# Router, slot table and first weight units reordered in a one-core retention, latent-attention and expert trunk

## The reference, cut to what matters

```python
# h_res: 16 meta tokens + 256 frames, D_MODEL 1024, two layers, float32
for layer in range(2):
    hn = rms_norm(h_res, attn_norm[layer])
    r_q, r_k, r_v, r_g, c_q, c_kv, k_rope = split(hn @ w_in[layer])
    y_ret = head_rms(retention(rope(r_q) * 128**-0.5, rope(r_k), r_v)) * ret_out_gain[layer] * silu(r_g)
    y_mla = head_rms(latent_attention(c_q, c_kv, k_rope, ...)) * mla_out_gain[layer]
    h_res = h_res + concat([y_ret, y_mla]) @ w_out[layer]
    hn = rms_norm(h_res, ffn_norm[layer])
    if layer == 0:
        h_res = h_res + (silu(hn @ w_gate) * (hn @ w_up)) @ w_down          # D_FF 3584
    else:
        top_val, top_idx = top_k(hn @ router_w, 2)                          # 8 experts
        gates = softmax(top_val)
        for e in range(8):
            h_res = h_res + gate_dense[:, e] * (silu(hn @ w_gate[e]) * (hn @ w_up[e])) @ w_down[e]
out = rms_norm(h_res, final_norm)[:, 16:]
```

## Time and profile before

| | us |
|---|---|
| median of 3 runs | 1513.21 (1512.12 to 1514.98) |
| profiled execution, its own time | 1514.2 |
| its span, first to last instruction | 1512.4 |
| PE busy | 1486.0 (98%) |
| DVE / ACT / POOL busy | 1229.4 / 1007.2 / 44.3 |
| 16 transfer engines moving | 445.89 MB, mean 295 GB/s |
| chain that ended last | PE 92%, DVE 4%, ACT 2%, DMA 1%, issue 1% |

### The profile page before, as it was taken

The page is one execution under the profiler, slowest core; times in us unless marked ns, Lnnn a source line. Parts: engine busy times, 40 slices in busy tenths (PEclk is TensorE's granted clock), DMA queues, the critical chain, the costliest instruction groups (busy, mean ns, idle before and its releaser), DMA issues.

```text
span 1512.4 us, 21641 instructions
## 1 busy us (share of the span) xinstructions
PE 1486.0 (98%) x8278; PEld 1289.0 (85%) x8278; DVE 1229.4 (81%) x1055; ACT 1007.2 (67%) x939; POOL 44.3 (3%) x44
## 2 busy tenths in 40 slices
PE   9999999999999999999999999999999999999997
PEld 8779999999988888888888888888888888888885
DVE  6746776777784678888898898888889888888887
ACT  7656433333575567777777777777777777777775
POOL 0000000000000031000000000000000000000000
PEclk9999999999999999999999999999999999999999
DMA  9305544444323469999999999999999999999992
GB/s 356 123 36 223 194 168 172 185 174 167 124 106 141 168 228 391 383 369 402 380 350 403 379 348 403 391 345 393 398 349 383 400 377 353 408 373 345 421 383 101
DMA packets 64857, 445.89 MB, mean 295 GB/s; under 512 B 8137, under 2 KB 8169, under 8 KB 12832
## 3 DMA queue, kind: packets, MB, share of 16 engines
q1 hardware_dynamic: 61344, 435.39, 73.4%
q0 software_dynamic: 3456, 9.71, 2.3%
HBM read 440.10 MB, written 7.36 MB: 296 GB/s over the span
## 4 chain that ended last, share of the span: by engine, by line
PE 92%; DVE 4%; ACT 2%; DMA 1%; issue 1%; SPq 0%; DVEq 0%; ACTq 0%
PE bank L524 89%; PE bank L528 3%; DVE w_lo L1320 1%; DMA ring<-stream 1%; ACT w_hi L998 0%; DVE scratch L1382 0%; ACT scratch L1076 0%; DVE scratch L1378 0%; DVE scratch L1367 0%; DVE scratch L1371 0%; ACT scratch L1075 0%; DVE scratch L1384 0%; DVE scratch L1527 0%; DVE scratch L1647 0%; DVE w_lo L1655 0%
## 5 line engine op out<-in xcount | busy, mean ns | idle before, releaser
L524 PE MATMUL bank<-w_hi,parts 128*128 128x512 f32 x2688 | 833.7, 391 | 1.5 <-issue 0.8
L1655 DVE TENSOR_TENSOR w_lo<-ring,w_hi 128x2048 fp32r<-128x2048 f32 x285 | 653.3, 2292 | 87.6 <-ACT w_hi L1220 84.2
L1220 ACT ACTIVATE w_hi<-ring 128x2048 fp32r<-128x2048 f32 x285 | 546.9, 1919 | 173.7 <-PE bank L524 146.4
L524 PEld LDWEIGHTS bank<-w_hi,parts 128*128 128x128 f32 x2688 | 500.3, 188 | 103.5 <-DVE w_lo L1655 1.1
L524 PE MATMUL bank<-w_lo,parts 128*128 128x512 f32 x1344 | 523.7, 390 | 0.0
L524 PE MATMUL bank<-parts,w_hi 128*128 128x272 f32 (+1 forms) x2240 | 427.3, 289 | 2.0 <-DVE w_lo L1320 1.9
L524 PEld LDWEIGHTS bank<-parts,w_hi 128*128 128x128 f32 x2240 | 351.6, 188 | 4.3 <-DVE w_lo L1320 2.5
L524 PE MATMUL bank<-parts,w_lo 128*128 128x272 f32 (+1 forms) x1120 | 321.3, 287 | 0.0
L524 PEld LDWEIGHTS bank<-w_lo,parts 128*128 128x128 f32 x1344 | 252.3, 188 | 53.1
L524 PEld LDWEIGHTS bank<-parts,w_lo 128*128 128x128 f32 x1120 | 211.0, 188 | 0.3
L1320 DVE TENSOR_TENSOR w_lo<-ring,w_hi 128x2048 fp32r<-128x2048 f32 x72 | 163.5, 2288 | 49.4 <-ACT w_hi L998 49.3
(11 more groups left out here) (187 smaller groups left out, 626.6 us busy)
## 6 DMA issues: line engine op xcount, KB each, us to landing
ring<-stream SPq DMA_DIRECT2D x357, 1024.0 KB, 6.1
hT<-stream SPq DMA_DIRECT2D x48, 1024.0 KB, 6.5
ring<-stream SPq DMA_DIRECT2D x4, 512.0 KB, 5.6
ring<-stream SPq DMA_DIRECT2D x2, 976.0 KB, 4.6
ring<-stream SPq DMA_DIRECT2D x2, 768.0 KB, 11.6
c_sb<-consts SPq DMA_DIRECT2D x1, 1136.0 KB, 11.1
hT<-h SPq DMA_DIRECT2D x4, 272.0 KB, 6.2
ring<-stream SPq DMA_DIRECT2D x2, 544.0 KB, 6.1
```

The lines of the kernel that those rows point to most:

```text
L524: return release(nc.tensor.matmul(dst, lhsT, rhs, start=start, stop=stop), inc)
L1220: A(w_hi[:, n % HSLOTS, :], moe_slot(m), ACT.Copy).then_inc(split_hi, 1)
L1655: V.tensor_tensor(w_lo[:, n % HSLOTS, :], moe_slot(m), w_hi[:, n % HSLOTS, :].bitcast(F32), ALU.subtract).then_inc(split_lo, 1)
```

## The change

It has four parts.

1. **Start.** Unit 1 is loaded, rounded and subtracted in two halves, as unit 0 was (`load_half(u, j)`, `high_half`, `low_half`), and PE's `cq0` begins on the first half. Unit 2 is loaded ahead of the constants. `keep_clock` is 21 instead of 24.
2. **Both attentions.** `square_sum` follows `cq1` instead of `cq0`, ACT evicts `cq0` and `cq1` before `row_root`. `low(b+6)` and `low(b+7)` leave the run of ropes: one goes behind `rope(10)`, one between the first two `mask_max`. `high(b+7)` goes behind `v2`. The fold of the eight squares is made in another order (`half_squares` first).
3. **Router.** The slot table has a third word, the token's 1/rms; `hn_rows` holds `res` without it, POOL's two multiplications and `hn_tok` are gone, and in passes 1 to 7 the scale enters in `Silu(scale=norm_now)` and in DVE's product (`scalar_tensor_tensor` with `slot_norm`); for pass 0 it is 1, since `G` holds 1/rms. ACT copies the scale of a pass to `norm_now` and waits for that. ACT squares the last two token blocks straight from PSUM before it copies them. DVE makes `G` and `G_last` before `gained(1)`, and takes the first rows (`take(0)`) ahead of the gate arithmetic. The counts of all experts go to bank 3 with a semaphore of their own (`total_done`). `keep_clock(5, 3)` stands before the counting and `keep_clock(2, 6)` behind it. POOL clears `x_rows` after two copies instead of four. `wo(7)` is parted in two with `logits(6, 7)` between. `scatter_copy` moves from the head of a pass to the end of the pass before, and falls away for pass 0.
4. **End.** The last two down units are used one by one, both halves of columns for each. The two last additions go before `fin_eps`; the last store is issued by ACT.

```diff
@@ SP, start @@
-            load_half(0)
+            load_half(0, 0)
             load_rows(0)
             load_rows(1)
-            load_half(1)
+            load_half(0, 1)
             load_rows(2)
             load_rows(3)
-            load(1)
+            load_half(1, 0)
+            load_half(1, 1)
+            load(2)
             sp.dma_start(c_sb[:, :], consts).then_inc(const_in, 16)
-            load(2)
...
@@ POOL, router @@
-            pool.wait_ge(tok_free, 4)
+            pool.wait_ge(tok_free, 2)
             nc.gpsimd.memset(x_rows, 0.0).then_inc(rows_set, 1)
             pool.dma_start(fn_sb, fnorm[:, 0, :]).then_inc(fn_in, 16)
             pool.wait_ge(gained_ready, 4)
-            pool.wait_ge(r_ready, 1)
-            for t in range(2):
-                nc.gpsimd.tensor_tensor(hn_tok[:, t, :], res[:, t, :], dev_tok[:, t, 3:4].to_broadcast([P, D]),
-                                        ALU.mult).then_inc(tokhn_ready, 1)
...
@@ PE, end of layer 1's attention @@
-                    wo(7, [*latent, *retained], True)
-                    logits(6, 8)
+                    wo(7, latent, False)
+                    logits(6, 7)
+                    wo(7, retained, True)
+                    logits(7, 8)
                     turn_tokens(1)
...
@@ ACT, turn_copies @@
+                copy(0)
+                copy(1)
+                square(0)
+                square(1)
+                A(warm[:, :], eps_sb[:, :], ACT.Sqrt)
+                square(2)
+                square(3)
+                copy(2)
                 act.wait_ge(tok_sum, 1)
                 A(dev_tok[:, :, 2:3], dev_tok[:, :, 2:3], ACT.Sqrt, bias=eps_sb[:, 0:1], scale=1.0 / D).then_inc(tok_std, 1)
+                copy(3)
...
@@ ACT, expert @@
-                scatter_copy(it)
+                A(norm_now[:, 0:1], slot_norm[:, it, :], ACT.Copy).then_inc(norm_set, 1)
+                act.wait_ge(norm_set, it + 1)
...
-                        A(sil_moe, bank[c % 2][:, :], ACT.Silu).then_inc(e_silu, 1)
+                        A(sil_moe, bank[c % 2][:, :], ACT.Silu, scale=norm_now[:, 0:1]).then_inc(e_silu, 1)
...
+                if not final:
+                    scatter_copy(it + 1)
...
@@ DVE, expert @@
-                        V.tensor_tensor(a_moe, bank[2 + c % 2][:, :], sil_moe, ALU.mult).then_inc(e_af, 1)
+                        V.scalar_tensor_tensor(out=a_moe, in0=bank[2 + c % 2][:, :], scalar=slot_norm[:, it, :], in1=sil_moe,
+                                               op0=ALU.mult, op1=ALU.mult).then_inc(e_af, 1)
...
@@ PE, last pass @@
                 def down_by_halves():
-                    for half in range(2):
-                        for f in range(4):
-                            i = f // 2
...
+                    for i in range(2):
+                        w = [x.rearrange("p (f n) -> p f n", f=2) for x in ready(("d", c, i))]
+                        for half in range(2):
+                            for ff in range(2):
```

175 lines of the change are left out of this document (95 added, 80 removed).

## The result

The changed kernel takes 1500.65 us (median of 4 runs, 1500.11 to 1501.44), the kernel before, run beside it, 1512.66 (1511.83 to 1514.98). The ratio is 0.9919, 95% interval 0.9901 to 0.9936: 0.8% faster. The profiled executions have spans of 1498.8 and 1512.4, 13.6 us apart; 1.5 us of that is the profiled execution of before, which took 1514.2 and so lay that far above its median.

What follows compares the result with a forecast made beforehand. PE, busy 1486.0 of 1512.4 us, was taken as the bound, so only its idling and low clock could be won. 5.0 + 0.7 + 1.9 + 1.9 + 2.8 + 0.4 = 12.7 us, from 1513.2 to 1500.5; range 1497.5 to 1505.0.

Steps and rivals of the forecast that it cites:

- Layer 0, start and ropes: Layer 0's attention: 1.3 us from an earlier root, 2.2 and 1.54 from moving two subtractions out of the ropes; 5.0 us.
- a lead for PE only: Layer 0's start: `cq0` starts about 1.9 us earlier, but DVE's unit 3 rest still stands behind `row_scale` and `rope(0)`.
- PE's wait before q2: Layer 0: PE stands still some 1.3 us before q2, costing nothing since the ropes end the stretch.
- Before the dense layer: Sum of squares before the dense layer: ready at 154.05 instead of 154.8; taken as 0.7 us, between 0 and 1.4.
- Layer 1's ropes: Layer 1's attention: 2.2 + 1.57 us from two moved subtractions, less 1.85 for the later root; gain 1.9 us.
- Layer 1's clock: Behind layer 1's ropes: with two of three waits gone PE's clock does not fall; 1.9 us, between 0 and 1.9.
- Router: Routing up to unit 3's rest in the first pass, which ends at 558.3 instead of 561.1; gain 2.8 us, bounds 0.9 to 4.2.
- The memset's term: Router: POOL's memset now runs beside DVE's `gained(0)`; cost taken as 0, at most 0.7 us.
- Passes: Expert passes: DVE's product at 0.74 instead of 0.68 us and ACT's new copy are both hidden; cost 0.
- End: Kernel's end: the 0.7 us wait for the last `w_lo` goes, second rest gains 0.3; taken as 0.4, -0.3 to 0.9.
- low clock stays: Layer 1's ropes and the gather keep the low clock, each costing 1.9 us: gain 8.9, time 1504.3; chance 0.20.
- The rival of the late unit 2: Start: unit 2 still lands at 19.7, root 1.2 us later, not 1.3 earlier: gain 10.2, time 1503.0; chance 0.10.

Runs made afterwards that it cites:

- e1: Changed kernel with both subtractions, `low(b + 6)` and `low(b + 7)`, put back among the ropes of both layers: 1511.03 us, ratio 0.9975 to before.
- e11: Changed kernel with unit 1 loaded, rounded and subtracted as a whole again, unit 2 still ahead of the constants: 1505.39 us, ratio 0.9940 to before.
- e4: Changed kernel with the sum of squares between cq0 and cq1 again and the root ahead of their evictions, both layers: 1498.76 us, ratio 0.9900 to before.
- e2: Changed kernel with only the first subtraction, `low(b + 6)`, put back among the ropes, in both layers: 1505.01 us, ratio 0.9944 to before.
- e10: Changed kernel with the last two down units used by halves of columns again: 1502.61 us, ratio 0.9921 to before.
- e9: Changed kernel with the last two additions of the residual behind `fin_eps` again: 1501.90 us, ratio 0.9918 to before.
- e5: Changed kernel without the seven matmuls of ones in the router: 1502.81 us, ratio 0.9927 to before.
- e3: Changed kernel with the constants loaded ahead of unit 2 again: 1505.11 us, ratio 0.9935 to before.

## Why the prediction was right

It named 1500.5 us and 12.7 us of gain; measured were 1500.65 and, between medians, 12.0, between the profiled spans 13.6. Term by term, against the marks:

- **Layer 0, start and ropes, 5.0.** Measured 5.02. The parts are 1.6 (start, said 1.3) and 3.4 (two subtractions, said 2.2 + 1.54 = 3.74); e1 gives the 3.4 back. Two errors of 0.3 cancel. One sentence of this step was wrong: that unit 1 in halves is a lead for PE only. With the sum behind cq1 the root needs that lead, and without it 3 us are lost (e11). The number survived because, with the halves, PE is done with cq1 at 21.16, 0.7 us before ACT comes to its bank. The 0.5 us for three matmuls of ones fewer were 0.37, and did not matter. PE's wait before q2 was 0.73 us, not 1.3.
- **Before the dense layer, 0.7.** Measured 0.81.
- **Layer 1's ropes, 1.9.** PE's last wait there ended at 450.84 before (the row below) and at 443.14 now, 7.70 us earlier, of which 5.83 came from before: 1.87. The loss by the later root was said to be 1.85; e4 shows 1.9 at the root and 1.19 at the ropes' end. e1 gives the two subtractions as 3.8 in this layer (said 3.77), and 3.8 less 1.9 is the 1.87. The 1.19 is what the root is worth once the subtractions are gone; two savings on the way to the same end don't simply add.

```profile
450.84 2.12 PE L524 MATMUL bank<-scratch,ring 128*128 128x272 f32 x4 [0.98 <-ACT scratch L1076]
```

- **Layer 1's clock, 1.9.** A1 gained 9.38, so 1.7 came from here. The trace shows 1.00 where there was 0.50. The reason given, that two of three waits were gone, is not supported: e1 has four waits there, e2 three, and no fall at that place. The term came true without its reason, which is luck as far as these runs tell; why the kernel before fell there stays open.
- **Router, 2.8.** Measured 12.31 - 9.38 = 2.9. The steps hold too: `gained(1)` was forecast to free the right half of the gather at 546.35 in the old kernel's time, and 536.97 + 9.38 is 546.35; that is also when PE is done with the left half. `G`'s pair took 0.60 (said 0.5), PE began the pass 4.9 earlier (said 4.2) and waited 1.84 at unit 3 (said 1.2), which ends at the same time. The memset's term, taken as 0, is 0 as far as the rows show: `gained(0)` took 1.29 beside it as it did without it.
- **Passes, 0.** From U3 to PE's last transposition it takes 930.08 us, 0.2 more than before. The product costs 0.75 instead of 0.68 and nobody waits for it.
- **End, 0.4.** Measured 1.5, from the last transposition on: the step that failed. Its 0.3 for the units one by one was somewhat small (0.5 in e10), but the additions ahead of `fin_eps` had no term of their own. The rows of before showed it: DVE idle 0.87 us in front of that instruction while two additions stood behind it (e9, 0.9 to 1.0).

The rival "low clock stays" did not come true in the changed kernel, and e5 shows that the seven matmuls of ones are what kept it away in the router. But the low clock came back at a place where I had put a wait and no price: at unit 3, in five of ten traces, 1.5 us each. None of the four executions of the changed kernel seems to have it (mean granted clock 0.998 in all), which is luck too; with it the time would have been about 1502.2, still within the range. The sum should have held "a new wait of 1.2 us, and perhaps 1.5 for the clock behind it". That a fall may come there and may not is the widest uncertainty left in this kernel, as the 941.3 to 941.5 against 939.7 to 939.8 us show. The rival of the late unit 2 had its price right: e3 makes unit 2 late, at 2.45 us, where the sum had 2.5.

## What to carry to other kernels

When a large engine is full and only short stretches can be won, follow each one's queue instruction by instruction and ask what is last after the edit; sums made so held within 0.3 us at six of seven places here. Give every instruction that changes its place its own term, the tiny ones too, when large ones are queued behind them. And price a new wait of the matrix engine twice, by its length and by what a fall of the clock behind it may cost; here, small arithmetic moved into an idle gap of 1.6 us took the wait away.
